# Sample queries against new retention states: bf16 products in three parts, summed ahead of the norm

## The reference, cut to what matters

```python
def retention(q, k, v, s0):     # q, k, v: (b, t, H, d); s0: (b, H, d, d); H = 8 heads, d = 128
    ...
    def step(s, blk):
        qc, kc, vc = blk
        sc = jnp.einsum('bnhd,bmhd->bhnm', qc, kc) * decay[None]
        o_in = jnp.einsum('bhnm,bmhe->bnhe', sc, vc)
        o_cross = jnp.einsum('bnhd,bhde->bnhe', qc, s) * xi[None, :, :, None]
        s_new = g_c[None, :, None, None] * s + jnp.einsum('bmhd,bmhe->bhde', kc * zeta[None, :, :, None], vc)
        return s_new, o_in + o_cross
    ...
mu = jnp.mean(o, axis=-1, keepdims=True)               # over the 128 channels of a head
var = jnp.mean(jnp.square(o - mu), axis=-1, keepdims=True)
o = (o - mu) * lax.rsqrt(var + GN_EPS)                 # then gain, bias and silu(g) * o
```

## Time and profile before

| | us |
|---|---|
| median of three runs | 2143.92 |
| the profiled execution, device time | 2143.7 |
| its span, first to last instruction | 2142.1 |
| TensorE busy | 2119.1 (99%) |
| VectorE busy | 1421.5 (66%) |
| ScalarE busy | 941.1 (44%) |

### The profile page before, as it was taken

How to read it: one execution, slowest core, us unless ns; L and a number is a source line. 1 busy time by engine, 2 the same in 40 slices (tenths; PEclk the granted TensorE clock), 3 DMA queues, 4 the chain that set the end, 5 groups by cost and what they waited for, 6 DMA issues and landing times.

```text
span 2142.1 us, 46352 instructions
## 1 busy us (share of the span) xinstructions
PE 2119.1 (99%) x18553; PEld 2101.1 (98%) x18553; DVE 1421.5 (66%) x2684; ACT 941.1 (44%) x1303; POOL 59.7 (3%) x78
## 2 busy tenths in 40 slices
PE   8999999999999999999999999999999999999997
PEld 7999999999999999999999999999999999999997
DVE  7667776568888667754656566666655556666665
ACT  6454433444444434444434343444434344444444
POOL 1000000000010000000000000000000000000000
PEclk9999999999999999999999999999999999999999
DMA  7555555654455556675656665656656566666553
GB/s 276 178 188 179 181 166 179 201 184 151 154 188 181 184 173 217 208 237 194 201 183 213 193 215 184 212 194 201 205 194 202 178 206 212 205 209 206 199 178 127
DMA packets 113767, 414.17 MB, mean 193 GB/s; under 512 B 13216, under 2 KB 13728, under 8 KB 113344
## 3 DMA queue, kind: packets, MB, share of 16 engines
q1 hardware_dynamic: 100800, 365.29, 52.6%
q0 software_dynamic: 8480, 30.24, 4.4%
q10 hardware_dynamic: 4320, 16.22, 1.9%
HBM read 387.36 MB, written 24.26 MB: 192 GB/s over the span
## 4 chain that ended last, share of the span: by engine, by line
PE 98%; DVE 1%; ACT 0%; DMA 0%; issue 0%; DVEq 0%; SPq 0%; ACTq 0%
PE bank L881 31%; PE bank L882 31%; PE bank L883 31%; PE bank L1058 2%; PE bank L959 1%; PE bank L1013 1%; PE bank L948 0%; PE bank L969 0%; DVE wlo L1137 0%; DMA acc<-xT 0%; PE bank L946 0%; DVE acc L1785 0%; PE bank L936 0%; PE bank L965 0%; ACT whi L612 0%
## 5 line engine op out<-in xcount | busy, mean ns | idle before, releaser
L1137 DVE TENSOR_TENSOR wlo<-raw,whi 128x1024 fp32r<-128x1024 f32 x688 | 829.9, 1223 | 537.7 <-ACT whi L612 534.4
L612 ACT CAST whi<-raw 128x1024 fp32r<-128x1024 f32 x688 | 709.6, 1048 | 646.0 <-PE bank L883 636.8
L881 PE MATMUL bank<-xhi,whi 128*128 128x264 f32 x3200 | 911.5, 285 | 0.0
L882 PE MATMUL bank<-xlo,whi 128*128 128x264 f32 x3200 | 906.7, 283 | 0.0
L883 PE MATMUL bank<-xhi,wlo 128*128 128x264 f32 x3200 | 906.5, 283 | 0.0
L882 PEld LDWEIGHTS bank<-xlo,whi 128*128 128x128 f32 x3200 | 603.1, 188 | 0.0
L881 PEld LDWEIGHTS bank<-xhi,whi 128*128 128x128 f32 x3200 | 602.6, 188 | 0.2 <-issue 0.2
L883 PEld LDWEIGHTS bank<-xhi,wlo 128*128 128x128 f32 x3200 | 600.1, 188 | 0.0
L881 PE MATMUL bank<-xghi,whi 128*128 128x264 f32 x1152 | 333.6, 290 | 11.2 <-DVE wlo L1137 11.2
L881 PE MATMUL bank<-wexp_hi,whi 128*128 128x264 f32 x1152 | 328.0, 285 | 0.0
L882 PE MATMUL bank<-xglo,whi 128*128 128x264 f32 x1152 | 327.4, 284 | 0.0
(11 more groups left out here) (215 smaller groups left out, 1102.2 us busy)
## 6 DMA issues: line engine op xcount, KB each, us to landing
raw<-halves SPq DMA_DIRECT2D x688, 512.0 KB, 3.5
hid<-gates ACTq DMA_DIRECT2D x30, 528.0 KB, 4.6
gates<-stage POOLq DMA_DIRECT2D x17, 768.0 KB, 7.1
s_old<-ret_state POOLq DMA_DIRECT2D x8, 512.0 KB, 6.0
ret_sample<-s_new POOLq DMA_DIRECT2D x8, 512.0 KB, 4.1
gates<-route_mem POOLq DMA_DIRECT2D x5, 768.0 KB, 7.2
acc<-xT SPq DMA_DIRECT2D x4, 528.0 KB, 6.4
tables<-shape_constants POOLq DMA_DIRECT2D x1, 1584.0 KB, 8.3
```

The lines of the kernel that those rows point to most:

```text
L612: nc.scalar.copy(whi[:, s], raw[:, s]).then_inc(hi_done, 1)
L881: nc.tensor.matmul(out, whi[:, s, c], mh[c], start=start and c == 0, stop=False)
L882: nc.tensor.matmul(out, whi[:, s, c], ml[c], start=False, stop=False)
L1137: v.tensor_tensor(wlo[:, s], raw[:, s], whi[:, s].bitcast(F32), ALU.subtract).then_inc(lo_done, 1)
```

## The change

The new states of the samples and the sample queries are each split into three bf16 numbers whose sum is the float32 number (a float32 has 24 bits of mantissa, a bf16 has 8). Per sample TensorE now does three products of 128 x 128 by 3 columns, in one accumulation: part n of the state against the three parts of the query. All nine products are formed; the three columns of a sample are added up by VectorE. In detail:

- ScalarE, `state_parts`: four casts of 128 x 512, between `state1` and `swap(1)`: the first bf16 part from `s_new`, the second from the rest, in two halves each.
- VectorE, `new_states`: four subtractions of 128 x 512 more (`s_rest`, then the third part), each waiting for a cast of ScalarE. `snew_ready` counts halves, so GpSimd waits for twice the number.
- VectorE, `query_parts`: four chained instructions of 128 x 8 behind the rotation of the query, ahead of `deviation`.
- VectorE, `sample_outputs`: a reduction of bank 6, 24 columns to 8, into `oT`. ScalarE's copy into `oT` is cut to the 256 prompt columns.
- VectorE's order: `ahead(r, 2)`, which stood behind `normed` and `gates_out`, now stands ahead of them, with `sample_outputs` behind it. The wait for `o_done` goes there too.
- TensorE: `outputs` waits for `q_parts_ready` and `s_parts_ready`, `mean` waits for `os_ready` also.

```diff
@@ scalar
+            def state_parts(p):
+                for sem_, of, need, done in ((snew_ready, s_new, 0, s_part1), (s_rest1, s_rest, 1, s_part2)):
+                    for t in range(2):
+                        act.wait_ge(sem_, 2 * p + t + 1)
+                        some = slice(4 * t, 4 * t + 4)
+                        nc.scalar.copy(s_parts[:, need, some], of[:, some]).then_inc(done, 1)
...
                     nc.scalar.copy(state1[:], bank[7][:, 0:P]).then_inc(s1_ready, 1)
+                    state_parts(h - 1)
@@ tensor
-                pe.wait_ge(snew_ready, p + 1)
+                pe.wait_ge(q_parts_ready, p + 1)
+                pe.wait_ge(s_parts_ready, 2 * p + 2)
                 for b in range(NSAMPLE):
-                    mm = nc.tensor.matmul(bank[6][:, NPROMPT + b:NPROMPT + b + 1], s_new[:, b],
-                                          qT[:, NPROMPT + b:NPROMPT + b + 1], start=True, stop=True)
+                    at = NPROMPT + PARTS * b
+                    for n in range(PARTS):
+                        mm = nc.tensor.matmul(bank[6][:, at:at + PARTS], s_parts[:, n, b], q_parts[:, b],
+                                              start=n == 0, stop=n == PARTS - 1)
                 mm.then_inc(o_done, 1)
...
             def mean(p):
                 pe.wait_ge(o_ready, p + 1)
+                pe.wait_ge(os_ready, p + 1)
@@ vector
+                for t in range(2):
+                    some = slice(4 * t, 4 * t + 4)
+                    dve.wait_ge(s_part1, 2 * p + t + 1)
+                    v.tensor_tensor(s_rest[:, some], s_new[:, some], s_parts[:, 0, some], ALU.subtract)\
+                        .then_inc(s_rest1, 1)
+                for t in range(2):
+                    some = slice(4 * t, 4 * t + 4)
+                    dve.wait_ge(s_part2, 2 * p + t + 1)
+                    v.tensor_tensor(s_parts[:, 2, some], s_rest[:, some], s_parts[:, 1, some], ALU.subtract)\
+                        .then_inc(s_parts_ready, 1)
+
+            def query_parts(p):
+                dve.wait_ge(rot_ready, p * 2 + 2)
+                ch.did(v.tensor_copy(q_parts[:, :, 0], qT[:, NPROMPT:T]))
+                ch.wait()
+                ch.did(v.tensor_tensor(q_rest[:], qT[:, NPROMPT:T], q_parts[:, :, 0], ALU.subtract))
+                ch.wait()
+                ch.did(v.tensor_copy(q_parts[:, :, 1], q_rest[:]))
+                ch.wait()
+                v.tensor_tensor(q_parts[:, :, 2], q_rest[:], q_parts[:, :, 1], ALU.subtract).then_inc(q_parts_ready, 1)
+
+            def sample_outputs(p):
+                dve.wait_ge(o_ready, p + 1)
+                v.tensor_reduce(oT[:, NPROMPT:T], bank[6][:, NPROMPT:NPROMPT + PARTS * NSAMPLE]
+                                .rearrange("p (s n) -> p s n", n=PARTS), AX.X, ALU.add).then_inc(os_ready, 1)
...
                 if att:
                     new_states(h - 1)
+                if loads_tiles(h) and not first:
+                    ahead(r, 2)
+                if att:
+                    dve.wait_ge(o_done, h)
+                    sample_outputs(h - 1)
                 if norm:
                     normed(h - 2)
                 if att:
                     gates_out(h - 1)
-                if loads_tiles(h) and not first:
-                    ahead(r, 2)
                 if tiles:
...
-                if att:
-                    dve.wait_ge(o_done, h)
                 if tiles:
                     tile_done(r, 2)
                     rotate(qT, 2, "cosq", "sinq", h * 2 + 1)
+                    query_parts(h)
```

## The result

The changed kernel takes 2162.78 us, the median of six runs (2161.8 to 2163.51); the kernel before, on the same chip, 2144.02 (2143.17 to 2144.35). The ratio is 1.0088, with a 95% interval of 1.0076 to 1.0099. The profiled execution took 2161.99 us with a span of 2160.4, against 2143.7 and 2142.1: 18.3 us more. The forecast was 2158.3.

A forecast was written before the change was run, and what follows sets the result against it. TensorE, 99% busy, was the bound, with an equally long chain over ScalarE and VectorE. Six heads at 2.39 us (14.3), plus 0.5, less 0.4, gave 2158.3 against the median; range 2153 to 2167, from its own terms 2154 to 2164.

The forecast's parts named there:

- The two chains of 6.27 us: From tile 2's end to the variance, TensorE's chain and the one over ScalarE and VectorE both take 6.27 us.
- The products: Sample products on TensorE: 24 bf16 products take 0.72 us instead of 1.68, saving 0.96 us a head.
- Do the parts come in time?: State casts and subtractions on ScalarE and VectorE end at 109.36, just before TensorE's products at 109.73; cost 0 to 0.4 a head.
- The order: On VectorE, low halves ahead of norm and gate delay the key's rotation, so `swap(2)` starts 1.56 us later a head.
- The query's parts: Four VectorE instructions between the query's rotation and the deviation lengthen the chain to the variance by 0.83 us a head.
- TensorE's waits: In each pass TensorE idles 0.9 us ahead of tile 3 for the gate and 2.4 us ahead of the variance.
- Head 1 and head 8: Outside heads 2 to 7: head 1, without norm, gets 0.5 us longer; head 8, without rotation, 0.4 us shorter.
- The clock: Rival: TensorE's clock falls to 1.2 GHz behind the new gaps, 1.9 us each, 11.7 us on top, 2170; chance 0.08.
- My own sign of being wrong: On TensorE, products behind the gap ahead of the variance standing 0.22 us apart would show the forecast wrong.
- late casts: Rival on ScalarE: state casts delay `swap(1)` by 0.4 us a head, giving 2161; inside the forecast's range, no separate chance.
- a dear reduction: VectorE's `sample_outputs` taking its upper bound of 0.43 us instead of the 0.20 assumed.
- dearer query's parts: The query's parts on VectorE costing their upper bound of 1.0 us a head instead of 0.83.

The follow-up runs named there:

- the fastest order: Changed kernel with the norm split around VectorE's wait and the low halves, query's parts behind the deviation: 2137.17 us, ratio 0.9971 to the kernel before.
- the kernel with the filled wait: Changed kernel plus 24 unused bf16 products ahead of TensorE's wait for the variance in heads 1 to 8: 2157.52 us, ratio 1.0065 to the kernel before.

## Why the prediction was right, and where it was off

- **The two chains of 6.27 us.** Right, and the root of all that follows. TensorE's saving is lost unless the chain over `swap(2)` gets shorter too (products back to float32 in the changed kernel: nothing in the loop; in the fastest order: 8.0 to 8.6 us).
- **The products.** 0.72 forecast from the batch of 64 columns, 0.61 measured: with 3 columns a product takes 0.025 us, load included. The lower bound of 0.3 us that I gave "if columns counted" does not follow (0.72 x 3/64 is 0.03), and nothing hung on it. The general rule of the Trainium skill for loads ("TensorE: Matmul & The Clock Gate", "LDWEIGHTS (loading the stationary operand)") would have given an estimated 2.6 us; the trace sides with the same page's exception for fast weight loads.
- **Do the parts come in time?** Right. Third parts were forecast to end 4.06 us behind the start of `s_new` (109.36 less 105.30); they end 4.15 behind it (112.15 less 108.00), and the products start without a wait. `swap(1)` is released by tile 1.
- **The order.** 1.56 forecast, 1.46 by the trace (31.59 less 29.30 less 0.83). I had put 0.20 on the sums and 0.40 on the gate; the rows have 0.09 (115.94 to 116.03) and 0.34. The norm's 3.81 came out to the digit. The order alone in the kernel before costs 1.36; the sums make up 0.09 of the difference.
- **The query's parts.** 0.83 forecast, 0.83 measured (1.18 less 0.35), and 0.83 by taking them off the chain (31.59 less 30.76).
- **TensorE's waits.** 0.9 forecast ahead of tile 3 and 1.0 measured; 2.4 forecast ahead of the variance and 2.1 measured.
- **Head 1 and head 8.** +0.5 and -0.4 forecast. Measured +0.4 by the variance of head 1; -0.6 behind that of head 7 if the stretch at the lower clock costs 1.6 there.
- **The clock.** Named as a rival with a chance of 0.08, and priced at 1.9 us a fall in all six passes. It came in three passes of the profiled execution, 1.6 us each: 4.8 us, the whole distance between 2158.3 and 2162.8. 2162.8 less 4.8 is 2158.0, and the kernel with the filled wait is at 2157.5. My own sign of being wrong, products 0.22 us apart behind the gap, is in the trace in these three passes. The mechanism was named; what failed was the weight I gave it. I had argued that the gap is a quarter of the one at the start, and no row of the kernel before shows what the clock does behind a gap of that size.

The range of 2153 to 2167 was meant to take in a clock that falls in some passes, and that is what happened. The narrower range worked out from the forecast's own terms, 2154 to 2164, holds the measured 2162.8 too, but that is luck: its upper end is made of late casts, a dear reduction and dearer query's parts, none of which came, and the price of the clock is not in it.

## What to carry to other kernels

Look for the second chain before pricing a saving: where two engines reach a meeting point within 0.1 us of each other, what one of them saves is worth nothing, and what the other gets on top is paid in full. Instructions that filled an unavoidable wait are not free to move. Here nine instructions ran while VectorE would have waited for ScalarE, and putting two others ahead of them left that wait empty and cost 1.4 us a pass; the reverse, putting work of the length of the wait into it (three instructions, 1.4 us, in a wait of 1.5), made the change pay. And work that only a later stage needs goes behind the instruction that the next engine waits for, not ahead of it.

## What the runs showed of the hardware

- TensorE's granted clock fell to the lower level behind waits of 2.1 us in three passes of six in the changed kernel, and in three of six with float32 products too; not once behind waits of 1.7, 1.3, 0.8 or 0.3 us in the other runs. It was about 3.4 us at that level each time, and each cost 1.6 us. In both kernels it was every second pass. Why not each one stays open; no run tells it.
- In the pass looked at the fall begins behind the wait, not in it: the variance at 128.56 and the transposes up to 129.7 still ran at full pace, and the tile's products behind them stood 0.22 us apart.
- A reduction of 24 columns in PSUM to 8 took 0.17 us on VectorE, and the next instruction started 0.09 behind it. A cast of 512 columns to bf16 on ScalarE took 0.65 from start to start (108.78 to 109.43). Two float32 subtractions of 512 columns with a bf16 operand took 1.35 on VectorE; the two float32 instructions of the same size ahead of them (L1270) took 1.40.
